# Memory products of both layers first, weight landings in the written order, conditioning pieces off the branch projections

## What is computed

```
def mixer_layer(x, mem, layer_idx, ...):
    h = rmsnorm(x, g_norm)
    dq, dk, dv, dg, lq, lk, lv, lg, mq, mg, mgate = split(h @ w_in)
    y_a = (rmsnorm(diff_attention(dq, dk, dv)) * silu(dg)) @ w_br_diff
    y_b = (softmax-weighted sum of 3 dilated groups(lq, lk, lv) * silu(lg)) @ w_br_dil
    kv  = rmsnorm(mem, g_mem) @ w_mem_kv          # mem is the same in both layers
    y_m = (memory_attention(mq, kv) * silu(mg)) @ w_br_mem
    gates = sigmoid(mgate)                        # three of width 1024
    return x + (gates[0]*y_a + gates[1]*y_b + gates[2]*y_m) @ w_out
```

## Time and profile before

| | |
|---|---|
| median of 3 runs | 2316.07 us (2310.77 to 2317.88) |
| the profiled execution | 2312.43 us, its span 2310.6 us |
| TensorE, matmuls busy | 2176.4 us, 94% |
| VectorE busy | 1567.7 us, 68% |
| ScalarE busy | 1029.3 us, 45% |
| GpSimd busy | 179.6 us, 8% |
| moved by DMA | 474.55 MB, mean 205 GB/s |

### The profile page before, as it was taken

One profiled execution on the slowest core, in us unless ns is written; L12 is line 12 of the kernel. 1 busy time (PEld: TensorE's weight loads), 2 busy tenths in 40 slices (PEclk: granted clock), 3 DMA queues, 4 the chain that ended last, 5 costly groups with the idle time before them and its releaser, 6 DMA issues. The chain is left out here.

```text
span 2310.6 us, 33985 instructions
## 1 busy us (share of the span) xinstructions
PE 2176.4 (94%) x13827; PEld 1936.8 (84%) x13827; DVE 1567.7 (68%) x2153; ACT 1029.3 (45%) x1698; POOL 179.6 (8%) x200
## 2 busy tenths in 40 slices
PE   6999998799999997989999999999999999999997
PEld 5999887678998885768899887899898889778996
DVE  5576576665766585765898767899744896656544
ACT  4444454344444553445443453434445434454433
POOL 1000010100000000011001100001100001111000
PEclk8999999899999998999999999999999999999998
DMA  8867455585776454643699643699643697535561
GB/s 287 264 204 243 151 166 195 174 280 181 223 231 200 143 170 172 240 141 97 210 329 319 225 139 101 213 342 342 221 150 128 227 352 248 180 107 164 189 204 64
DMA packets 296816, 474.55 MB, mean 205 GB/s; under 512 B 19904, under 2 KB 151434, under 8 KB 296660
## 3 DMA queue, kind: packets, MB, share of 16 engines
q1 hardware_dynamic: 286548, 440.67, 56.5%
q0 software_dynamic: 10112, 31.71, 4.7%
HBM read 465.88 MB, written 6.42 MB: 204 GB/s over the span
## 5 line engine op out<-in xcount | busy, mean ns | idle before, releaser
L150 DVE TENSOR_TENSOR wlo<-raw,whi 128x1024 fp32r<-128x1024 f32 x640 | 774.1, 1239 | 194.8 <-ACT whi L144 192.8
L144 ACT ACTIVATE whi<-raw 128x1024 fp32r<-128x1024 f32 x640 | 646.7, 1055 | 286.0 <-DMA raw<-in_ffn_w_gu 100.4
L138 PE MATMUL G<-HTh,whi 128*128 128x256 f32 x2304 | 661.6, 287 | 11.8 <-ACT pool L144 5.9
L138 PE MATMUL G<-HTh,wlo 128*128 128x256 f32 x2304 | 651.8, 283 | 0.0
L138 PE MATMUL G<-HTl,whi 128*128 128x256 f32 x2304 | 651.7, 283 | 0.0
L138 PEld LDWEIGHTS G<-HTh,whi 128*128 128x128 f32 x2304 | 441.5, 192 | 20.3 <-issue 13.9
L138 PEld LDWEIGHTS G<-HTl,whi 128*128 128x128 f32 x2304 | 441.7, 192 | 2.0
L138 PEld LDWEIGHTS G<-HTh,wlo 128*128 128x128 f32 x2304 | 441.4, 192 | 0.0
L144 ACT ACTIVATE pool<-G 128x512 f32<-128x512 f32 (+2 forms) x208 | 115.5, 573 | 553.7 <-PE G L138 519.5
L138 PE MATMUL G<-whi,HTh 128*128 128x512 f32 (+1 forms) x768 | 310.3, 404 | 19.5 <-ACT HTh L144 11.8
L138 PE MATMUL G<-whi,HTl 128*128 128x512 f32 (+1 forms) x768 | 300.6, 391 | 4.1 <-DVE HTl L158 4.0
(11 more groups left out here) (195 smaller groups left out, 2314.4 us busy)
## 6 DMA issues: line engine op xcount, KB each, us to landing
raw<-in_ada_w SPq DMA_DIRECT2D x192, 512.0 KB, 5.9
raw<-in_ffn_w_gu SPq DMA_DIRECT2D x352, 256.0 KB, 4.9
raw<-in_w_in SPq DMA_DIRECT2D x128, 512.0 KB, 4.6
raw<-in_ffn_w_down SPq DMA_DIRECT2D x88, 512.0 KB, 6.5
raw<-in_w_in SPq DMA_DIRECT2D x160, 256.0 KB, 4.3
pool<-mod_rows POOLq DMA_DIRECT2D x24, 512.0 KB, 6.6
raw<-in_swa_w_in SPq DMA_DIRECT2D x24, 512.0 KB, 5.7
raw<-in_gla_w_in SPq DMA_DIRECT2D x24, 512.0 KB, 5.1
```

The source lines that it names most:

```text
L138: return self.e.matmul(out, a, b, start=start, stop=stop, skip_group_check=True) if self.e else self
L144: return self.e.activation(out, a, func, bias=bias, scale=scale, accum_out=accum) if self.e else self
L150: return self.e.tensor_tensor(out, a, b, op) if self.e else self
```

## The change

Layer 1's memory keys and values are made at the start, behind layer 0's; their pieces move in the list from behind `yb` to the front. The memory rows are normalized twice from one load, into two places, and the gain row of layer 1 is loaded in `setup`. The squares of x, its mean, rows and transposes are written among the memory products, through `soon`, a list of things to do a given number of pieces later. Layer 1's keys and values are stored to DRAM after the first projection and loaded again at the start of layer 1, on GpSimd's queue.

In `spread` the gates, `ym` and `yb` are excluded from getting conditioning pieces. The first stack gets 66 instead of 72, the feed-forward parts of the second 46, 48 and 32 instead of 40, 44 and 36.

A piece gets a landing time on the order's clock: 1.6 us after the one before it, and at least 4.5 us after its buffer was read. Splits and conditioning pieces are placed no earlier, and `urgent` stops at one that has not landed. `gbank` goes by the age of a bank (last taken or emptied) instead of round robin.

```diff
@@ Memory.__init__ @@
+        self.kvs = nc.dram_tensor("kv_scratch", (2, P, D), F32, kind="Internal").ap()
@@ layer1_pieces @@
     if l == 0:
         mkv(0)
+        mkv(1)
...
-    if l == 0:
-        mkv(1)
@@ spread @@
-          and main[i][1][0] not in ("diff", "swa", "gla", "fox", "wo2") for i in range(len(main))]
+          and main[i][1][0] not in ("diff", "gate", "ym", "yb", "swa", "gla", "fox", "wo2") for i in range(len(main))]
@@ weight_stream @@
-    res = spread(layer1_pieces(I, 0) + layer1_pieces(I, 1), ada(0) + ada(1)[:24], 12, 24)
+    res = spread(layer1_pieces(I, 0) + layer1_pieces(I, 1), ada(0) + ada(1)[:18], 10, 24)
     for l in range(4):
-        extra = (ada(1)[24:] + ada(2)[:16], ada(2)[16:] + ada(3)[:12], ada(3)[12:], [])[l]
+        extra = (ada(1)[18:] + ada(2)[:16], ada(2)[16:] + ada(3)[:16], ada(3)[16:], [])[l]
@@ gbank @@
-            g = min((self.bclk[g], (g - self.gnext) % 4, g) for g in range(4) if not self.gheld[g])[2]
-            self.gnext, self.bclk[g] = g + 1, max(self.bclk[g], self.clk["PE"]) + 0.7
+            g = min((self.bclk[g], self.gage[g], g) for g in range(4) if not self.gheld[g])[2]
+            self.gage[g], self.bclk[g] = max(self.gage) + 1, max(self.bclk[g], self.clk["PE"]) + 0.7
             return g
-        while self.gheld[self.gnext % 4]:
-            self.gnext += 1
-        g = self.gnext % 4
-        self.gnext += 1
+        g = min((self.gage[g], g) for g in range(4) if not self.gheld[g])[1]
+        self.gage[g] = max(self.gage) + 1
         return g
@@ fetch @@
+        p.land = self.landed = max(self.landed + 1.6, self.freed[r] + 4.5)
@@ split, rest1, ada @@
-        p.ends = self.spend("ACT", 1.05)
+        p.ends = self.spend("ACT", 1.05, p.land)
...
-        self.spend("DVE", 1.24, p.ends)
+        self.freed[p.r] = self.spend("DVE", 1.24, p.ends)
...
-        self.spend("DVE", 1.5)
+        self.freed[p.r] = self.spend("DVE", 1.5, p.land)
@@ urgent @@
+                if p[0].ends is None and p[0].land > self.clk["ACT"] + 0.3:
+                    return
@@ filling @@
-        res += [(self.clk["ACT"], "ACT", p) for p in first]
+        res += [(max(self.clk["ACT"], p.land), "ACT", p) for p in first]
...
-                    res.append((self.clk["DVE"], "DVE", p))
+                    res.append((max(self.clk["DVE"], p.land), "DVE", p))
@@ evacuate @@
-        self.gfree[b], self.gheld[b] = evac(g, self.M.GB[b], full), False
+        self.gfree[b], self.gheld[b], self.gage[b] = evac(g, self.M.GB[b], full), False, max(self.gage) + 1
@@ mem_kv @@
+    def mem_kv(self):
+
+        memb, b0 = self.memb, self.mk_blk(8)
+        d0 = self.mem_rows(memb.a, b0.a, self.gm[0], [self.tmem] + b0.w)
+        b0.release(self.to_T(lambda t: b0.a[:, t * D:t * D + D], [[[x] for x in d] for d in d0], self.HT))
+        d1 = self.mem_rows(memb.a, memb.a, self.gm[1], [d0[1][1]])
+        N = Norm(self, self.gn)
+        for t in range(2):
+            for u in range(2):
+                self.square(N, t, u, self.M.X[:, t, u * 512:u * 512 + 512], self.tx, self.mk_blk(2))
+            N.nx[t].append(self.tx)
+        self.mkvb = [{"k": self.mk_blk(4)}]
+        used = self.gemm(self.HT, 0, ("mkv", 0, 0), D, "FF", self.ev_copy(self.mkvb[0]["k"]))
+        self.write_scratch(used)
+
+        def mem1(t, c):
+            def f():
+                g, tr = self.tr4(memb.a[:, t * D + c * 512:t * D + c * 512 + 512], [d1[t][c]])
+                self.split_tr(t, c, g, self.OT, None, tr)
+                if t and c:
+                    memb.release([tr])
+            return f
+        self.soon += [[1 + 2 * t + c, mem1(t, c)] for t in range(2) for c in range(2)]
+        self.mkvb[0]["v"] = self.mk_blk(4)
+        self.gemm(self.HT, 0, ("mkv", 0, 1), D, "TT", self.ev_copy(self.mkvb[0]["v"]))
+        make = self.normed(N)
+        part = [make(0), make(1)]
+        self.soon += [[1 + 2 * t + c, lambda t=t, c=c: part[t](c)()] for t in range(2) for c in range(2)]
+        B = [self.mk_blk(4), self.mk_blk(4)]
+        self.gemm(self.OT, 0, ("mkv", 1, 0), D, "FF", self.ev_copy(B[0]))
+        self.gemm(self.OT, 0, ("mkv", 1, 1), D, "TT", self.ev_copy(B[1]))
+        return B
@@ layer1 @@
+            kv1 = self.mem_kv()
             b4, first = self.layer1_head(0)
...
+            self.parked = [self.load("POOL", f"kv{i}", M.kvs[i], b.a, b.tok) for i, b in enumerate(kv1)]
+            for i, b in enumerate(kv1):
+                b.release([self.parked[i]])
         else:
             b4 = self.b4
-        B = self.mkvb.pop(0)
+            self.mkvb = [{"k": self.mk_blk(4), "v": self.mk_blk(4)}]
+            for i, b in enumerate(self.mkvb[0].values()):
+                b.tok = [self.load("POOL", f"kvb{i}", b.a, M.kvs[i], b.w + [self.parked[i]])]
+        B = self.mkvb[0]
```

More of the change, by code:

```diff
@@ L255, in __init__ @@
     def __init__(self, i, r, ld, n, ada):
-        self.i, self.r, self.ld, self.n, self.ada, self.ends = i, r, ld, n, ada, None
+        self.i, self.r, self.ld, self.n, self.ada, self.ends, self.land = i, r, ld, n, ada, None, 0
 class Memory:
@@ L436, in __init__ @@
             sl.j = j
-        self.gfree, self.gheld, self.gnext = [[] for _ in range(4)], [False] * 4, 0
+        self.gfree, self.gheld, self.gage = [[] for _ in range(4)], [False] * 4, [0] * 4
         self.pfree, self.pbusy = [[] for _ in range(NB)], [False] * NB
@@ L442, in __init__ @@
         self.piece, self.half, self.halves, self.adaq, self.held, self.steps = 0, 0, [], [], 0, 0
-        self.raw_free, self.todo = [[] for _ in range(NRAW)], []
+        self.raw_free, self.todo, self.freed, self.landed = [[] for _ in range(NRAW)], [], [-9] * NRAW, -9
         self.spl_free = [[] for _ in range(NSPL)]
@@ L1272, in mem_kv @@
             for c in range(2):
-                x = mb[t][:, c * 512:c * 512 + 512]
-                self.h_rows(x, x, M.rmem[:, t:t + 1], gm.a[:, c * 512:c * 512 + 512], ALU.mult,
-                            [ready[t], self.trmem[t]] + gm.tok, done[t][c])
-        rel = self.to_T(lambda t: mb[t], [[[x] for x in d] for d in done], self.OT)
+                w = slice(t * D + c * 512, t * D + c * 512 + 512)
+                self.h_rows(dst[:, w], src[:, w], self.M.rmem[:, t:t + 1], gm.a[:, c * 512:c * 512 + 512], ALU.mult,
+                            [self.trmem[t]] + ready + gm.tok, done[t][c])
@@ L1277, in mem_kv @@
         gm.release([done[1][1]])
-        for b in blks:
-            b.release(rel)
-        B = {"k": self.mk_blk(4)}
-        used = self.gemm(self.OT, 0, ("mkv", l, 0), D, "FF", self.ev_copy(B["k"]))
-        if l == 0:
-            self.write_scratch(used)
-        B["v"] = self.mk_blk(4)
-        self.gemm(self.OT, 0, ("mkv", l, 1), D, "TT", self.ev_copy(B["v"]))
-        self.mkvb.append(B)
+        return done
+    def mem_kv(self):
[28 more added lines that the diff above has]
+        return B
@@ L1295, in layer1 @@
         if l == 0:
-            mb = self.memb
-            self.mem_kv(0, [mb.a[:, t * D:t * D + D] for t in range(2)], [mb], [self.tmem] * 2)
             self.xtok = [[self.tx], [self.tx]]
-            N = Norm(self, self.gn)
-            for t in range(2):
-                for u in range(2):
-                    self.square(N, t, u, M.X[:, t, u * 512:u * 512 + 512], self.tx, self.mk_blk(2))
-                N.nx[t].append(self.tx)
-            make = self.normed(N)
-            for t in range(2):
-                part = make(t)
-                for f in [part(0), part(1)]:
-                    f()
+            kv1 = self.mem_kv()
             b4, first = self.layer1_head(0)
@@ L1421, in layer1 @@
             gb = gate_of(1, u)
-            if u == 1 and l == 0:
-                mb = [self.mk_blk(4), self.mk_blk(4)]
-                self.gm = self.row_gain("gm1", I["g_mem"][1])
-                tm = [self.load("POOL", f"mem1{t}", mb[t].a, I["mem"][0][t * P:t * P + P, :], mb[t].w)
-                      for t in range(2)]
             y_of(("yb", l, u), 4, 512, u, gb, False)
-        if l == 0:
-            self.mem_kv(1, [b.a for b in mb], mb, tm)
         blocks["free"] = True
@@ L1546, in sit @@
         self.live[:], self.seats, self.spare = [None] * len(self.place), True, spare
-        self.pairs, self.slack = pairs, slack
+        self.pairs, self.slack, self.freed, self.landed = pairs, slack, [-9] * NRAW, -9
         self.clk, self.bclk = {"PE": 0, "DVE": 0, "ACT": 0}, [0] * 8
```

7 lines of the change are left out of this document (3 added, 4 removed).

## The result

| | before | after |
|---|---|---|
| median of 4 runs, us | 2313.57 (2310.77 to 2317.88) | 2259.47 (2258.98 to 2260.08) |
| profiled run: span / whole, us | 2310.6 / 2312.4 | 2257.2 / 2258.98 |
| mean granted TensorE clock | 0.980 | 0.989 |
| TensorE busy, us (13,827 matmuls in both) | 2176.4 | 2161.0 |
| TensorE's waits, summed, us | 119.0 | 80.6 |

The ratio is 0.9765, with a 95% interval of 0.9746 to 0.9783: 54 us faster, where 37 had been forecast. The time lies 2.5 us under the lower end of the range. The last two rows of the table make up the gain: 38.4 us less waiting and 15.4 us less busy time for the same number of matmuls make 53.8, and the span fell by 53.4.

A forecast was written before the change was run, and what follows sets the result against it. TensorE was taken to bound the kernel, idling in the branch stretches behind late weight loads. The terms summed to -36.9 us from 2312.4, giving 2275.5, plus 3.6 for the median: 2279 us, range 2262 to 2312.

The forecast's parts named there:

- What bounds the kernel: Gate and branch projections: conditioning pieces hold raw buffers, so weight loads, splits and copies come late; TensorE idles 38.7 us.
- Branch stretches, -18 and -15: Gates and branch projections of layers 0 and 1: most TensorE idle goes without conditioning pieces, -18 and -15 us.
- x's norm, -8.9: Between memory products and first projection: idle of 7.4 us and 1.5 us of half clock go, -8.9 us.
- Start, +3.0: Before the first product: x's squares on ScalarE and layer 1's memory rows on VectorE come ahead, +3.0 us.
- Dilated stretches, +4: Dilated stretches of both layers: 60 conditioning pieces instead of 39, three per four weights, cost +4 us.
- the rival's 2.4: Price of 2.4 us for each of 21 more conditioning pieces in the dilated stretches, giving 2325 us; chance 0.14.
- Feed-forward +2, layer 2 -4: Feed-forward parts: more conditioning pieces in layers 0 and 1 cost +2 us, fewer in layer 2 save 4 us.
- Parking 0: GpSimd's queue: storing layer 1's memory keys and values to DRAM and loading them again costs 0, bounds 0 to +5.
- The units' own chain: Branch stretches: attention units' own chain makes the gaps, not the buffer ring; half of 33 us stays, 2295 us, chance 0.18.
- The dilated stretches catch the loss: Dilated stretches: eight buffers no longer hold the look-ahead, splits wait for landings, slower at 2325 us; chance 0.14.
- the sign I had named: Dilated stretches: SyncE's waits for conditioning pieces grown past those of 362 to 443 would show the prediction wrong.
- Transfers cap the feed-forward parts: Feed-forward of layers 0 and 1: transfers limited to 346 GB/s, 8 us instead of 2, 2284 us; chance 0.10.

The follow-up runs named there:

- the forced taking: Kernel before, with VectorE made to take a conditioning piece when the load four places behind it is fetched, instead of eight: 2260.51 us, 0.9767.
- both experiments on it: Kernel after with 44 and 36 conditioning pieces again in layers 1 and 2, 2266.04 us; kernel before with VectorE's conditioning sums made short, 2301.82 us.
- without landings: Kernel after with every landing time set to 0, the rest as it is: 2257.57 us, 0.9755.
- spread alone: Kernel before with only the list changed: no conditioning pieces in gates, ym and yb, counts 66, 46, 48 and 32: 2256.05 us, 0.9748.

## Why the prediction was off, step by step

The forecast was 2279 us and the result is 19.5 us below it. 3.1 of these belong to the median: I had added 3.6 us to get from a profiled run to it, and it was 0.5. The other 16.5 are the terms. **The step that failed is the price of the two branch stretches**: I had -18 and -15 us for what measured -59.9 with the last gates behind them. The mechanism in it held; its idle time, its clock and the work that moves with it were mis-sized, as the second item says. Two further terms, layer 2's feed-forward and the stages that I had given nothing, came out 9.3 us too small. Against these 36.2 us stand 19.7 by which the start, the norm, the first projection, the dilated stages and the other feed-forward parts came out worse than I had reckoned. So it is luck that the forecast was no further off: two kinds of error, each larger than what was left, had opposite signs.

- **What bounds the kernel** held: raw buffer held by a conditioning piece, load late, split late, copy behind the split. The link that was missing is why the buffer is held, which the forced taking settled: no due time, not a slow sum. And the order, which I had counted into the same terms, can give some 16 us without the ring, but not the rest.
- **Branch stretches, -18 and -15: mechanism right, size wrong.** Measured with the last gates: -32.3 and -27.6 us. *Idle*: I left 4 us in layer 0 and 2.6 in layer 1 for what "remains", where 0.05 remained, and put the stretch behind at 0, where the last gates had 2.5 us of idle that went too (the earlier trace rows showed 6.1 us in 443 to 533): 9.0 us. *Clock*: I counted 1 us, or none, where the same matmuls got shorter by 2.5 and 3.7 us in the gate stretches and 3.3 in layer 1's last gate (0.90 and 0.92 to 1.00): 8.5 us. *Work that only moved*: layer 1's transposes, 3.6 us, and six conditioning sums of TensorE, 5.7 us, which I had nowhere in the sum. The last shows in a view of tile ones alone, busy time of TensorE by stretch, first the gate stretch and the dilated stage of layer 0 before, then that stage after:

```profile
336.28:442.49 106.21, 1.89 (x16) 2.09 (x16) 0.00 (x0) 0.90 0.56 191
91.21:222.84 131.63, 3.80 (x32) 3.93 (x32) 0.00 (x0) 1.00 0.70 227
```

```profile
123.96:261.09 137.13, 6.65 (x56) 6.87 (x56) 0.00 (x0) 1.00 0.73 243
```

- **x's norm, -8.9**: memory of both layers together went from 63.45 to 55.50, -8.0, with those 3.6 us of transposes now inside, so -11.6 on the same footing. The gaps of the earlier trace rows closed. In my term 3.8 us at half rate should have been 1.9 us lost, not 1.5.
- **Start, +3.0**: +3.95. The squares of ScalarE did stand ahead of the split; with the squares and layer 1's rows put back, 2.8 of it returned.
- **First projection: missing from the sum, +8.2.** What failed here is the list of what a step issues. I followed the parking's stores and loads and gave the DRAM part a 0, but not the bias write that stands on the same queue. Before, the eight loads of the first projection were issued from 20.4 to 24.2 us, ahead of the write; with layer 1's memory pieces in front of them in the list they are issued from 50.4 to 75.4, under it. Closing a gap of TensorE took away the cover of a transfer that had been free. The 8.2 us are as much as the norm and memory had gained (8.0).
- **Dilated stretches, +4**: +12.4 with the first differential stage, for 21 more pieces, 0.6 us each. That is three times my figure and a quarter of the rival's 2.4. Half of it is no wait: TensorE's busy time in these stages grew by 6.3 us, 5.7 of them the six sums above (8 matmuls and 0.95 us each), and its idle by 6.1. I had counted what a piece costs VectorE, for ten more in layer 0 where the list gives eleven, and not what it costs TensorE.
- **Feed-forward +2, layer 2 -4**: +3.1 and -6.45. For layer 2 I went by TensorE's waits for VectorE (5.5 us), while the gap per block follows VectorE's busy 87.61 of 90; both experiments on it give 6, which is VectorE's time for four pieces.
- **Parking 0**: never alone, but memory first with all that belongs to it, parking and banks too, costs 1.5 us in sum by the medians (without landings 2257.57, against 2256.05 for spread alone), which is within what these runs can tell. The choice of bank by age was not measured by itself.
- **The rivals.** *The units' own chain* fell: the same units ran with 0.05 us of idle as soon as the ring was free. *The dilated stretches catch the loss*: the sign I had named was there, SyncE's waits for conditioning pieces in 101 to 261 us are 49.9 us, the longest 12.5, against 47.3 in the earlier trace rows, and yet TensorE idles only 4.9 of 160 us. Why a held ring costs so little there is open. *Transfers cap the feed-forward parts*: not at 346; the 120 us row above moved 357 GB/s with TensorE full, and the price was 1.3 us in layer 1. I hadn't named the one that did come: a transfer laid bare.

In sum, with my terms against the measured ones: +3.0 / +3.95 start, -8.9 / -8.0 norm and memory, 0 / +8.2 first projection, -33 / -59.9 branch stretches with what follows them, +4 / +12.4 dilated, +2 / +3.1, -4 / -6.45; the other stages together give some -7: output products of the second kind of layer -0.6 to -1.2 in each of four, the projection behind the last gate of layer 1 -1.0, layer 2's attention -0.9, layer 3's -1.85.

## What to carry to other kernels

Background work that shares a ring of buffers with urgent work needs a due time of its own, well ahead of the moment when its buffer is wanted; shortening it or shrinking its transfer doesn't help while it holds its place. When a stall goes, price it from the first to the last matmul of the stage, with the clock it costs and the stage behind it, and not by the idle time alone. And before you close a gap, list what was in flight under it: a large write that was free there will be paid for at the next loads.

## What the runs showed of the hardware

- A load of 256 or 512 KB that lands in about 5 us by the page's medians took 20 to 31 us beside one 5 MB write to DRAM (those issued between 50 and 65 us), while the two together moved some 193 GB/s (38 to 86 us), far below the 335 and 357 of the rows above. The Trainium skill, "DMA: Bandwidth & Descriptors", section Queues, rings and completion order, says that each DMA engine takes turns between the queues it has work for; the trace agrees so far as a load never waits for the whole write, yet is slowed four to six times.
- Cutting that write from one of 20 source partitions into ten of 2 made each of them last 26 to 56 us, for a tenth of the bytes. The same page of the Trainium skill, section Why a DMA increments its semaphore by 16 and not by 1, has the number of engines follow from the slowest dimension (the largest number up to 16 that divides it on both sides): an estimate by that is 10 engines for the one write and 2 for each of the ten. Each engine would then carry half as much as with the one write, and half of its 46.4 us is 23; the three writes issued first, which had least before them, took 26 to 27. The trace agrees so far; no view here shows the engines one by one.
- The clock followed the gaps: idle times of 5.9 to 8.5 us in the gate stretches went with 0.90 and 0.92, and the first projection, with an idle of 2.11 us right before it and one of 6.55 in it, ran at 0.76 over 21 us.
